# A hybrid trunk with an 8-expert layer: residual rows kept unscaled, the list of extra experts made in two parts, the short strip's remainder and a wait on the logits' operands put elsewhere

## What is computed

```
ALPHA = (2 * DEPTH) ** 0.25
...
            x = layer_norm(ALPHA * x + out, p['ln_c_g'][j], p['ln_c_b'][j])
            moe = moe_swiglu(x, p['moe_router'][j], p['moe_w1'][j], p['moe_w3'][j], p['moe_w2'][j])
            x = layer_norm(ALPHA * x + moe, p['ln_moe_g'][j], p['ln_moe_b'][j])
...
    probs = jax.nn.softmax((x @ router).astype(f32), axis=-1)
    top_p, top_e = lax.top_k(probs, TOP_K)
    top_p = top_p / jnp.sum(top_p, -1, keepdims=True)
...
        return (jax.nn.silu(xb @ w1[e]) * (xb @ w3[e])) @ w2[e]
...
    y = jnp.zeros((n_tok, d), f32).at[slot_token].add(y_slots)
```

## Time and profile before

| | before |
|---|---|
| time, median of 3 runs | 1557.72 us (1556.31 to 1558.15) |
| the profiled execution: its own time | 1557.08 us |
| its span | 1555.3 us |
| PE busy | 1461.1 us, 94% |
| DVE busy | 1187.4 us, 76% |
| ACT busy | 947.2 us, 61% |
| moved by transfers | 372 MB, mean 239 GB/s |

### The profile page before, as it was taken

How to read it: one execution, slowest core, us unless ns; L and a number is a source line. 1 busy time by engine, 2 the same in 40 slices (tenths; PEclk the granted TensorE clock), 3 DMA queues, 4 the chain that set the end, 5 groups by cost and what they waited for, 6 DMA issues and landing times.

```text
span 1555.3 us, 28933 instructions
## 1 busy us (share of the span) xinstructions
PE 1461.1 (94%) x11140; PEld 1307.5 (84%) x11141; DVE 1187.4 (76%) x1609; ACT 947.2 (61%) x1242; POOL 75.4 (5%) x149
## 2 busy tenths in 40 slices
PE   8989989899999899999999999999999999999992
PEld 7878989799999798988878887888878888788881
DVE  5664787655544668867798898988989899888994
ACT  4454135533333568555867877778777787768872
POOL 8200000000000000000000000000000000000000
PEclk9989999899999999999999999999999999999996
DMA  8511003344444343223889999999999999999972
GB/s 245 163 55 59 4 4 123 108 139 160 141 144 149 109 137 122 83 83 139 302 302 384 398 406 397 346 405 372 354 397 331 408 366 366 395 335 397 371 291 83
DMA packets 162175, 372.23 MB, mean 239 GB/s; under 512 B 10168, under 2 KB 85856, under 8 KB 162080
## 3 DMA queue, kind: packets, MB, share of 16 engines
q1 hardware_dynamic: 159408, 361.19, 63.3%
q0 software_dynamic: 2304, 8.39, 2.1%
q10 hardware_dynamic: 368, 1.31, 0.2%
HBM read 360.63 MB, written 10.24 MB: 238 GB/s over the span
## 4 chain that ended last, share of the span: by engine, by line
PE 73%; DVE 14%; issue 7%; ACT 3%; DMA 2%; DVEq 0%; SPq 0%; POOLq 0%; POOL 0%; ACTq 0%
PE bank L526 9%; PE bank L1150 9%; PE bank L1151 9%; PE bank L1152 9%; PE bank L527 9%; PE bank L528 9%; DVE w_lo L1896 6%; PE bank L618 4%; PE bank L1174 3%; PE bank L1175 3%; PE bank L1176 3%; DVE wd_lo L1231 1%; DMA moe_ring<-in_moe_w 1%; PE bank L931 1%; ACT wd_hi L2129 1%
## 5 line engine op out<-in xcount | busy, mean ns | idle before, releaser
L1896 DVE TENSOR_TENSOR w_lo<-moe_ring,w_hi 128x1024 fp32r<-128x1024 f32 (+1 forms) x560 | 609.7, 1159 | 40.4 <-ACT w_hi L2577 40.3
L2577 ACT ACTIVATE w_hi<-moe_ring 128x1024 fp32r<-128x1024 f32 (+1 forms) x560 | 532.3, 1014 | 93.3 <-PE bank L1176 50.1
L526 PE MATMUL bank<-in_hi,wd_hi 128*128 128x320 f32 x880 | 280.1, 318 | 20.4 <-DVE in_lo L1597 14.0
L1231 DVE TENSOR_TENSOR wd_lo<-arena,wd_hi 128x1024 fp32r<-128x1024 f32 x142 | 170.6, 1208 | 167.0 <-ACT wd_hi L2129 166.6
L1150 PE MATMUL bank<-w_hi,xe_hi 128*128 128x512 f32 (+1 forms) x768 | 288.5, 376 | 1.3 <-DVE w_lo L1896 1.3
L1151 PE MATMUL bank<-w_hi,xe_lo 128*128 128x512 f32 (+1 forms) x768 | 286.2, 373 | 0.0
L1152 PE MATMUL bank<-w_lo,xe_hi 128*128 128x512 f32 (+1 forms) x768 | 285.7, 372 | 0.0
L527 PE MATMUL bank<-in_lo,wd_hi 128*128 128x320 f32 x880 | 275.9, 314 | 0.0
L528 PE MATMUL bank<-in_hi,wd_lo 128*128 128x320 f32 x880 | 275.7, 313 | 0.0
L2129 ACT ACTIVATE wd_hi<-arena 128x1024 fp32r<-128x1024 f32 x142 | 147.7, 1046 | 174.9 <-PE bank L528 166.7
L526 PEld LDWEIGHTS bank<-in_hi,wd_hi 128*128 128x128 f32 x880 | 168.8, 192 | 25.0 <-issue 17.7
(11 more groups left out here) (401 smaller groups left out, 1711.0 us busy)
## 6 DMA issues: line engine op xcount, KB each, us to landing
moe_ring<-in_moe_w SPq DMA_DIRECT2D x216, 1024.0 KB, 8.2
moe_ring<-in_moe_w SPq DMA_DIRECT2D x64, 768.0 KB, 5.5
arena<-in_ffn_w SPq DMA_DIRECT2D x30, 1024.0 KB, 5.2
arena<-in_w_in_c SPq DMA_DIRECT2D x16, 1024.0 KB, 5.5
arena<-in_w_in_ab SPq DMA_DIRECT2D x13, 1024.0 KB, 6.1
arena<-in_w_out_ab SPq DMA_DIRECT2D x4, 1024.0 KB, 6.0
arena<-in_w_out_c SPq DMA_DIRECT2D x4, 1024.0 KB, 5.2
arena<-in_ffn_w SPq DMA_DIRECT2D x4, 768.0 KB, 4.4
```

The costliest lines, as they stand in the source:

```text
L526: pe.matmul(b[:, 0:T], w_[0][:, cols], x_hi, start=start, stop=False)
L1231: dve.tensor_tensor(wd_lo[:, m_ % DENSE_UNITS, 0:words], src, wd_hi[:, m_ % DENSE_UNITS, 0:words], ALU.subtract).then_inc(S("dense_lo"), 1)
L1896: dve.tensor_tensor(w_lo[:, i % UNITS, 0:unit_words(i)], moe_unit(i), w_hi[:, i % UNITS, 0:unit_words(i)], ALU.subtract)\
L2577: act.activation(w_hi[:, i % UNITS, 0:unit_words(i)], moe_unit(i), ACT.Copy).then_inc(S("e_hi"), 1)
```

## The change

Five edits. (1) The residual rows are no longer multiplied by ALPHA. Instead the weights of the experts' results are divided by it (one more operand in an instruction that was there), and the last norm's epsilon is divided by ALPHA squared, which gives the same rows after the norm: `residual_rows` goes. (2) With that, SP can store `y_rows` earlier: before piece 22 and not 28, and waiting for `x_whole`. (3) The list of extra blocks is made in two parts: `extra_experts` before the first expert's `xe_lo`, `extra_places` where `extras` was. (4) `hidden_rest(NS - 1)` stands behind unit 65 and not 67, on DVE alone and in every expert. (5) PE waits for the zeroed columns of `stats` not before the logits but before it turns them.

```diff
+LAST_AHEAD = 2
...
-ROW_UNITS, STORE_UNITS, BASE_UNITS, BASE_PIECE, LN_PIECE = [8, 10, 12, 14, 16, 18], [14, 18, 22], [38, 39, 40], 28, 33
+ROW_UNITS, STORE_UNITS, BASE_PIECE, LN_PIECE = [8, 10, 12, 14, 16, 18], [14, 18, 22], 22, 33
...
             b = take(("logit", 0), "logits_done", 1)
-            pe.wait_ge(*at_count("router_ready", 3))
+            pe.wait_ge(*at_count("router_ready", 2))
...
             pe.wait_ge(*at_count("logits_done", 1))
+            pe.wait_ge(*at_count("router_ready", 3))
...
-            link(dve.tensor_scalar(t3, t3, 1e-30, None, ALU.max))
+            link(dve.tensor_scalar(t3, t3, 1e-30, ALPHA, ALU.max, ALU.mult))
...
-            def extras():
+            def compacted(src, dst):
+                link(dve.tensor_tensor(compact[:, :, :], bc(cand[:, 1, :], 1, NX), bc(slots[:, 0:NX], 2, NX), ALU.is_equal))
+                link(dve.tensor_tensor(compact[:, :, :], compact[:, :, :], bc(cand[:, src, :], 1, NX), ALU.mult))
+                link(dve.tensor_reduce(cand[:, 4, :], compact[:, :, :], AX.X, ALU.add))
+                link(dve.tensor_copy(dst, cand[:, 4, :]))
+
+            def extra_experts():
                 for r_ in range(1, MAX_BLOCKS):
                     ins_ = dve.tensor_scalar(cand[:, 0, (r_ - 1) * NE:r_ * NE], cnt[:, :], BLK * r_ + 0.5, None, ALU.is_gt)
                 link(ins_)
...
+                compacted(2, extra_i[:, 0, :])
+
+            def extra_places():
+                compacted(3, bases[:, :])
                 link(dve.tensor_reduce(cand[:, 5, 0:1], cand[:, 0, :], AX.X, ALU.add))
                 dve.tensor_copy(n_extra[:, 0:1], cand[:, 5, 0:1]).then_inc(S("extras_known"), 1)
...
-            def residual_rows(i):
-                n = TILES[i][1]
-                dve.wait_ge(*at_count("x_rows_in", 48))
-                dve.wait_ge(*at_count("x_whole", i + 1))
-                dve.tensor_scalar(xtok[0:n, i, :], xtok[0:n, i, :], ALPHA, None, ALU.mult).then_inc(S("y0_done"), 1)
...
                         if i + 1 == U3_END[1]:
-                            extras()
-                    if i + 1 == DN_END[NS - 2] + AHEAD:
+                            extra_places()
+                    if i + 1 == DN_END[NS - 2] + LAST_AHEAD:
                         hidden_rest(NS - 1)
...
             for i in range(2, EARLY):
                 weight_rest(0, i)
+            dve.wait_ge(*at_count("pos_done", 2))
+            extra_experts()
...
-                            sp.wait_ge(*at_count("y0_done", i + 1))
+                            sp.wait_ge(*at_count("x_whole", i + 1))
```

More of the change, by code:

```diff
@@ L308, in mixed_trunk @@
         eps_norm = sb("eps_norm", [P, 1])
+        eps_out = sb("eps_out", [P, 1])
         lg = sb("lg", [P, 3, NE])
@@ L2059, in expert_block @@
                             rows_scaled(*divmod(ROW_UNITS.index(i), 2))
-                        if i in BASE_UNITS:
-                            residual_rows(BASE_UNITS.index(i))
                         if i + 1 == U3_END[1]:
-                            extras()
-                    if i + 1 == DN_END[NS - 2] + AHEAD:
+                            extra_places()
+                    if i + 1 == DN_END[NS - 2] + LAST_AHEAD:
                         hidden_rest(NS - 1)
@@ L2668, in _ @@
                 act.wait_ge(*at_count("y_var", i + 1))
-                link(act.activation(rstd[0:n, i, 0:1], mean_var[0:n, i, 1:2], ACT.Ln, bias=eps_norm[0:n, :]))
+                link(act.activation(rstd[0:n, i, 0:1], mean_var[0:n, i, 1:2], ACT.Ln, bias=eps_out[0:n, :]))
                 act.activation(rstd[0:n, i, 0:1], rstd[0:n, i, 0:1], ACT.Exp, scale=-0.5).then_inc(S("y_std"), 1)
@@ L2716, in _ @@
             link(pool.memset(eps_norm[:, :], NORM_EPS))
+            link(pool.memset(eps_out[:, :], NORM_EPS / ALPHA ** 2))
             link(pool.iota(slots[:, :], [[1, BLK]], base=0, channel_multiplier=0, allow_small_or_imprecise_dtypes=True))
```

## The result

The changed kernel takes 1540.57 us (median of 5 runs, 1539.99 to 1542.02), the kernel before 1557.72 (5 runs beside it, 1555.86 to 1558.55): a ratio of 0.9893, 95% interval 0.9879 to 0.9908. That is 1.1% faster. The forecast was 1541.6, with a range of 1539.0 to 1547.2. The profiled execution has a span of 1539.1 us, against 1555.3.

What follows compares the result with a forecast made beforehand. PE was taken as the bound, busy 94.58 of 95.62 us in a later expert. Gains of 9.1, 2.1, 2.5, 1.5 and 0.6, together 15.8 us off 1557.08, gave a forecast median of 1541.6 us, range 1539.0 to 1547.2.

Steps and rivals of the forecast that it cites:

- `gz_lo`, experts 2 to 8: Making `gz_lo` two units earlier on DVE removes PE's stall at unit 64, 1.30 us in each of seven experts: 9.1 us.
- `gz_lo`, first expert: The same earlier place removes PE's wait in the first expert: 2.1 us, or 1.2 if late weights hold DVE.
- List in two parts: At unit 32 of the first expert PE starts 2.5 us earlier, and 1.5 us more because the clock stays up.
- The clock's rival: The clock's part near unit 32 is not there to be won: 1.5 us less, 1543.1 us; chance 0.08.
- Router: PE begins the logits 0.9 us earlier, partly spent at half clock: 0.6 us, bounds 0.4 and 2.5.
- Residual rows: Dropping three DVE instructions around unit 39 gives nothing by itself but keeps DVE ahead: 0 us.
- Stores: Moving the `y_rows` stores ahead of pieces 22 to 27 shortens nothing PE waits for now: 0 us.
- the first rival: Transfers become the bound in the second expert, where PE waits for late weights: up to 5.5 us, 1547.1; chance 0.11.
- Sum: Over the whole kernel the terms 9.1, 2.1, 2.5, 1.5 and 0.6 give 15.8 us, for a forecast of 1541.6 us.
- Slower rival: DVE waits for `gz_hi` at the new place, remainders and PE queued behind: 1560.8 us; chance 0.02.

Runs made afterwards that it cites:

- gz_three: The changed kernel with the short strip's remainder (`hidden_rest(NS - 1)`) one unit later, behind unit 66: 1541.83 us, ratio 0.9903.
- undo_gz: The changed kernel with the short strip's remainder back behind unit 67, everything else as changed: 1550.49 us, ratio 0.9958.
- rows_back: The changed kernel with three multiplications of the same size, into a spare buffer, back behind units 38 to 40: 1540.78 us, ratio 0.9898.
- late_stores: The changed kernel with the `y_rows` stores back in front of piece 28 instead of 22: 1543.67 us, ratio 0.9914.
- gz_minus1: The changed kernel with the short strip's remainder three units earlier, behind unit 62: 1552.7 us, ratio 0.9969.
- gz_minus2: The changed kernel with the short strip's remainder behind unit 61: 1574.69 us, ratio 1.0118.
- only_gz: The kernel before with one edit alone, the short strip's remainder behind unit 65: 1547.52 us, ratio 0.9944.
- split_router: The changed kernel with the whole list of extra blocks behind unit 31 and PE waiting for the zeroed columns before the logits: 1545.86 us, ratio 0.9927.
- undo_split: The changed kernel with the whole list of extra blocks behind unit 31 again: 1542.78 us, ratio 0.9911.

## Why the prediction was right, point by point

- **`gz_lo`, experts 2 to 8: 9.1 us.** An expert went from 95.62 to 94.29, 7 x 1.33 = 9.3. The stall, its end by DVE's queue, the 0.18 us between `gz_hi` and DVE (0.19 measured) and the margin of 0.9 (0.96 by gz_three) all held.
- **`gz_lo`, first expert: 2.1 us.** The rest of B is 11.46 - 9.3 = 2.2, but it isn't all `gz_lo`'s. Undone alone (undo_gz), the place of `gz_lo` is worth 10.48 - 9.3 = 1.2 us there, which is the prediction's lower bound and its reason, late weights. The other 0.98 us is B of undo_gz against B of the kernel before, and goes with the stores.
- **List in two parts: 2.5 and 1.5 us.** 2.54 and 1.26. The place, the hidden 2.50 us ahead of `xe_lo` and the clock held in this pair of profiles. By the prediction 0.8 us of idle time would be left over in that cover (3.33 - 2.50); 1.78 were left, because the router's lead let DVE begin its remainders 1.58 us earlier (744.46, not 746.04), while `xe_lo` came only 0.77 earlier (752.10, not 752.87).
- **The clock's rival.** It had a chance of 0.08. The Trainium skill ("TensorE: Matmul & The Clock Gate", Part 1: The HAM clock gate) has it that the monitor runs free and the loss varies from run to run; here a wait of one length brought a fall in three of four executions, each of another kernel, and in seven of eight experts of one execution, so this case agrees as far as it goes: no kernel has two traces. By four executions alone the chance of "not there" would be a quarter; the 0.08 was low, and the term, 1.26 where it is won, is less as a mean.
- **Router: 0.6 us.** 0.78 to 0.84, and by the course foretold: the lead is partly spent at half speed. What the term lacked is that the small products at L1102 to L1108 now come ahead of the clock's fall and gain 0.6.
- **Residual rows: 0.** rows_back shows it.
- **Stores: 0, and the first rival.** This term was wrong, and it was luck that the sum held: the 0.98 us that the stores cost at the old pace was in the sum under `gz_lo` of the first expert. At the new pace their early place keeps 2.75 us (late_stores). The rival's place was right (late weights in the second expert), its other half, `gz_lo` late in the first, wasn't named. Its size with the stores left back, 5.5 - 4.0 = 1.5 by the prediction's figures, was too small by 1.25.
- **Sum.** 15.8 forecast, 16.06 in A and B, 16.2 in the spans. Its last step is off by 0.3 us: 1557.08 less 15.8 is 1541.3, and with the 0.6 us by which the median lies higher that gives 1541.9, not 1541.6.
- **Slower rival.** Its mechanism exists (gz_minus1, gz_minus2), and was seen three and four units ahead of the changed place; the two places between weren't tried.

## What to carry over

When a remainder or any small operation stands in an engine's queue ahead of a consumer's need, place it between two times read from the trace: not before its own input exists, not later than the consumer less the operation; here that interval was some 1.1 us wide, and the place inside it brought the whole gain. On the late side the first unit cost 0.17 us in every expert and the next 1.1 more. On the early side the third unit cost 1.4 and the fourth 2.8 more; the first two weren't tried. Price a moved transfer or store at the new pace, and look for its cost under the names of others: here late weights, 0.98 us before the changes and 2.75 behind them, showed as waits for `gz_lo` and `w_lo`. Idle time of an engine near a closed loop (PE frees the buffer, ACT fills it, DVE follows) isn't room for whatever delays the loop's start: 0.7 us of delay on the way into the loop cost 0.76. Moving 1.9 us of DVE's work into a pause gave 0.13, but together with a second edit.

## What the runs showed of the hardware

Equal waits don't cost the same. Behind waits of 2.46 to 2.73 us (eight in gz_minus2, one each in before, only_gz, split_router and undo_split) the granted clock fell from 2.4 to 1.2 GHz in ten of twelve places, and each fall cost 1.3 to 1.6 us of PE. Behind waits of 0.9 to 1.2 us (undo_gz and gz_minus1, eight each) it never fell, nor behind the one of 1.82 us in the kernel before.

The fall doesn't follow PE's restart at a fixed distance. In the kernel before PE resumes at 803.34 and the clock falls at 804.2. In gz_minus2 it falls at 840.7 in the first expert, 0.3 us before PE resumes, and at 1335.6 in the sixth, 1.4 us after PE resumes at 1334.20. These six falls come 99.0 us apart and the waits 98.5 to 98.7, so the distance grows from expert to expert, until behind the seventh wait the clock stays up. One pass of the same code can so differ from the next by 1.6 us (98.70 and 97.09).
